# Four logit buffers in the attention, a shorter router chain, output rows scaled at the copy out, projections into the convolution from the weighted residual

## The reference

```python
# attention of a head, keys s strictly before the query t
z = q.k / sqrt(64) + b_h
log_stay = where(causal, log_sigmoid(-z), 0)
between = reverse_cumsum(log_stay) - log_stay
weight = where(causal, exp(log_sigmoid(z) + between), 0)
o = weight @ v
# convolution module
a, g = split(rmsnorm(h) @ w_in)
u = a * sigmoid(g)
y = causal depthwise conv of u, width 31; layernorm; silu; @ w_out
# experts
y[t] = sum over the two chosen e of w_sel * (silu(x @ w_gate[e]) * (x @ w_up[e])) @ w_down[e]
# the end
y = rmsnorm(h, norm_final)
```

## Time and profile before

| | us |
|---|---|
| median of three runs | 1520.71 (1519.55 to 1520.96) |
| the profiled execution | 1512.51 |
| its span, first to last instruction | 1510.8 |
| PE busy | 1337.0 (88%) |
| DVE busy | 1022.6 (68%) |
| ACT busy | 702.9 (47%) |
| POOL busy | 239.7 (16%) |
| HBM traffic | 219 GB/s over the span |

### The profile page before, as it was taken

The page is one execution under the profiler, slowest core; times in us unless marked ns, Lnnn a source line. Parts: engine busy times, 40 slices in busy tenths (PEclk is TensorE's granted clock), DMA queues, the critical chain, the costliest instruction groups (busy, mean ns, idle before and its releaser), DMA issues. The chain is left out here.

```text
span 1510.8 us, 16104 instructions
## 1 busy us (share of the span) xinstructions
PE 1337.0 (88%) x6141; PEld 1044.2 (69%) x6142; DVE 1022.6 (68%) x1071; ACT 702.9 (47%) x685; POOL 239.7 (16%) x224
## 2 busy tenths in 40 slices
PE   2899899896699999998979999899489999998893
PEld 2686355585488878886768884578478878887772
DVE  3268944315798878885754999523598878885854
ACT  1010244114477768773620007223467767785532
POOL 1033321200213323210000000100112322211000
PEclk7899899997699999999989999999599999999996
DMA  6448436207489999986460302013279999994201
GB/s 258 181 175 350 152 133 251 59 1 279 135 320 374 303 374 376 373 334 238 138 223 0 112 16 100 3 34 109 71 270 386 386 303 388 389 371 180 111 0 57
DMA packets 122740, 314.05 MB, mean 208 GB/s; under 512 B 10060, under 2 KB 10720, under 8 KB 120608
## 3 DMA queue, kind: packets, MB, share of 16 engines
q1 hardware_dynamic: 106350, 249.82, 45.8%
q0 software_dynamic: 14256, 58.69, 10.8%
q10 hardware_dynamic: 2074, 4.71, 0.9%
HBM read 304.17 MB, written 26.70 MB: 219 GB/s over the span
## 5 line engine op out<-in xcount | busy, mean ns | idle before, releaser
L1727 PE MATMUL ps<-xnT,ring 128*128 128x260 f32 x1408 | 315.8, 388 | 13.0 <-DVE xnT L1207 7.1
L1727 PEld LDWEIGHTS ps<-xnT,ring 128*128 128x128 f32 x1408 | 271.9, 193 | 56.4 <-issue 14.4
L1958 PE MATMUL ps<-ring_parts,arena_parts 128*128 128x512 f32 x768 | 308.3, 401 | 0.0
L1478 DVE TENSOR_TENSOR ring_parts<-ring,xnT_parts 128x2048 fp32r<-128x2048 f32 x96 | 219.3, 2292 | 45.1 <-ACT xnT_parts L986 44.0
L1478 DVE TENSOR_TENSOR ring_parts<-ring,arena_parts 128x2048 fp32r<-128x2048 f32 x96 | 219.4, 2291 | 40.7 <-ACT arena_parts L986 40.4
L986 ACT ACTIVATE xnT_parts<-ring 128x2048 fp32r<-128x2048 f32 x96 | 183.5, 1917 | 85.3 <-PE ps L1959 76.7
L986 ACT ACTIVATE arena_parts<-ring 128x2048 fp32r<-128x2048 f32 x96 | 183.4, 1918 | 71.7 <-PE ps L1959 48.5
L1958 PEld LDWEIGHTS ps<-ring_parts,arena_parts 128*128 128x128 f32 x768 | 148.5, 193 | 31.1
L1957 PE MATMUL ps<-xnT_parts,arena_parts 128*128 128x512 f32 x384 | 159.1, 414 | 10.1 <-DVE arena_parts L1482 10.1
L1957 PE MATMUL ps<-arena_parts 128*128 128x512 f32 x384 | 155.5, 405 | 8.9 <-DVE arena_parts L1482 5.2
L1959 PE MATMUL ps<-xnT_parts,arena_parts 128*128 128x512 f32 x384 | 155.6, 405 | 0.0
(11 more groups left out here) (283 smaller groups left out, 1704.7 us busy)
## 6 DMA issues: line engine op xcount, KB each, us to landing
ring<-in_w_gate_e SPq DMA_DIRECT2D x32, 2048.0 KB, 16.5
ring<-in_w_up_e SPq DMA_DIRECT2D x32, 2048.0 KB, 16.8
ring<-in_w_down_e SPq DMA_DIRECT2D x32, 2048.0 KB, 17.6
ring<-in_w_in_ab SPq DMA_DIRECT2D x4, 2048.0 KB, 26.7
ring<-in_w_ple_gate SPq DMA_DIRECT2D x4, 2048.0 KB, 8.1
ring<-y_rows SPq DMA_DIRECT2D x16, 512.0 KB, 6.6
ring<-in_w_in_c SPq DMA_DIRECT2D x4, 2048.0 KB, 8.7
x_rows<-arena ACTq DMA_DIRECT2D x10, 416.0 KB
```

The lines of the kernel that those rows point to most:

```text
L1478: v.tensor_tensor(w_lo, w, high[hu0 % 4].bitcast(F32), ALU.subtract).then_inc(s_lo, 1)
L1727: ins = mm(s[:, half, 0:HALF], w[:, k, :], src[:, k, half * HALF:(half + 1) * HALF], start=(k == 0), stop=(k == n - 1))
L1958: mm(ps[:, bank, :], x, w_lo, start=False, stop=False)
```

## The change

Attention. The logit buffers become four: the fourth lies over the q and k of heads already used (q and k of a head pair lie side by side now), and `LOGIT_BUF` and `LOGIT_FREE` say which head takes which buffer and for how many heads' values it waits. POOL masks the softplus of head h before the weights of h-1, and adds ahead of the sticks what lies behind each key block: two copies of 128 columns, an add of 128 and an add of 384, with a wait on its own result after the mask and after the first add. The sticks become four triangle matmuls and three with ones, 2048 columns. `values` runs once for two heads, the two 64-column halves in turn. PE's order per head is scores(h+1), sample_values(h-2), at even h values of the pair before, [wait for the subtract of h-1] turn_sample(h-3), sticks(h).

Router, both layers. The sums of squares are made per token (`token_sums`, five matmuls of 104 tokens with one column of ones), the root is over 104x5 and the five turning matmuls go. The reciprocal comes before the wait for the turned logits. The rank takes five matmuls, the selection three broadcast operations, and the row indices are written and signalled (`s_rows_of`) before the other table columns; POOL waits for these only before its first scatter.

Into the convolution. ACT writes the residual weighted by the gain (`mixed`) while the embedding still runs; PE starts cg(0) from it, the square sums follow between cg(0) and ca(0), the history's transposes after ca(0). DVE drains cg, scaling it by the reciprocal root, ACT takes the sigmoid in place, DVE scales by the reciprocal root again before the product with ca. EARLY is 13.

End. ACT writes the weighted residual (`final_rows`) during the embedding of layer 1; PE begins the transposes of the first row group, with `token_sums` before the last of them; the root is over 128x4 and 8x1, ACT scales each row at the copy out, five row buffers, and the output DMAs go from POOL's queue to the end of SP's.

```diff
-EARLY = 15
+EARLY = 13
+LOGIT_BUF = (0, 1, 2, 0, 1, 3, 2, 0)
+LOGIT_FREE = (0, 0, 0, 2, 2, 0, 4, 4)
...
-    norm(3)
-    order += [("chist", i, "dve") for i in range(2)]
     for m in range(KT):
-        order += [("cg", m, "act"), ("ca", m, "dve")]
+        order.append(("cg", m, "dve"))
+        if not m:
+            norm(3)
+        order.append(("ca", m, "dve"))
+        if not m:
+            order += [("chist", i, "dve") for i in range(2)]
...
             for h in range(SBH):
+                pool.wait_ge(s_sp, h + 1)
+                sp, later = ex[:, h % 2, :], spare[h % 2]
+                link(mask(sp))
+                pool.tensor_copy(later[:, 0:P], sp[:, 1024:1024 + P])
+                pool.tensor_copy(later[:, 256:256 + P], sp[:, 512:512 + P])
+                link(pool.tensor_tensor(later[:, P:256], sp[:, 1024 + P:1280], sp[:, 896:1024], ALU.add))
+                pool.tensor_tensor(later[:, 256 + P:640], sp[:, 512 + P:896], later[:, 0:256], ALU.add
+                                   ).then_inc(s_spm, 1)
                 if h:
                     mask_weights(h - 1)
-                pool.wait_ge(s_sp, h + 1)
-                mask(ex[:, h % 2, :]).then_inc(s_spm, 1)
...
             for h in range(SBH):
                 if h + 1 < SBH:
                     scores(h + 1)
-                if h:
-                    values(h - 1)
+                if h >= 2:
+                    sample_values(h - 2)
+                    if h % 2 == 0:
+                        values(h // 2 - 1)
                 sticks(h)
...
-                if h >= 2:
-                    turn_sample(h - 2)
+                if h >= 3:
+                    turn_sample(h - 3)
                 pe.wait_ge(s_spm, h + 1)
...
                 for kb in range(4):
-                    for src in range(kb, 4):
-                        off = (src - kb) * P
-                        width = TP - src * P
-                        ins = mm(ps_flat[:, c0 + at[kb] + off:c0 + at[kb] + off + width],
-                                 tri[:] if src == kb else ones[:], sp[:, at[src]:at[src] + width],
-                                 start=(src == kb), stop=(src == 3), skip_group_check=True)
+                    col, width = c0 + at[kb], TP - kb * P
+                    ins = mm(ps_flat[:, col:col + width], tri[:], sp[:, at[kb]:at[kb] + width],
+                             start=True, stop=(kb == 3), skip_group_check=True)
+                    if kb < 3:
+                        ins = mm(ps_flat[:, col + P:col + width], ones[:], behind[kb],
+                                 start=False, stop=True, skip_group_check=True)
...
+            def values(p):
+                pe.wait_ge(s_wm, 2 * p + 2)
...
+                    for h in (2 * p, 2 * p + 1):
+                        rows = slice(64 * (h % 2), 64 * (h % 2) + 64)
...
+                ins.then_inc(s_pv, 2)
...
+            def token_sums(i, rows, count):
...
+                for n in range(count):
+                    last = min(T, (n + 1) * rows)
+                    ins = mm(s[0:last - n * rows, 0, n:n + 1], rstd[:, n * rows:last], ones[:, 0:1], start=True, stop=True)
...
-                for n in range(10):
-                    v.tensor_scalar(sel_c[:, n, :], iot, ten(15)[:, n:n + 1], None, ALU.is_equal)
-                    ins = v.tensor_scalar(sel_b[:, n, :], iot[:, 0:NE * BLK], ten(16)[:, n:n + 1],
-                                          vl[:, n:n + 1], ALU.is_equal, ALU.mult)
-                ins.then_inc(s_sel, 1)
+                link(v.tensor_tensor(sel_b, steps_of(NE * BLK), wide(ten(16), NE * BLK), ALU.is_equal))
+                v.tensor_tensor(sel_c, steps_of(CAP), wide(ten(15), CAP), ALU.is_equal)
+                v.tensor_tensor(sel_b, sel_b, wide(vl, NE * BLK), ALU.mult).then_inc(s_sel, 1)
...
                 for m in range(KT):
+                    s = drain_wait(dve, "cg", m)
+                    v.tensor_tensor(two(csig[:, m % 2, :]), halves(s), two(rstd[:]), ALU.mult
+                                    ).then_inc(s_drained["dve"], 1)
+                    if m:
+                        sample_sums(m - 1)
+                    dve.wait_ge(s_csig, m + 1)
+                    link(v.tensor_tensor(csig[:, m % 2, :], csig[:, m % 2, :], rstd[:], ALU.mult))
                     s = drain_wait(dve, "ca", m)
...
+            def final_rows(k):
+
+                nc.scalar.activation(xnT[:, k, :], hT[:, k, :], ACT.Copy, scale=prm[:, G_FIN + k:G_FIN + k + 1]
+                                     ).then_inc(s_hg, 1)
+
+            def mixed(k):
+
+                nc.scalar.activation(xnT[:, k, :], hT[:, k, :], ACT.Copy,
+                                     scale=prm[:, G_MIX + 8 + k:G_MIX + 9 + k]).then_inc(s_xn, 1)
...
             for i in range(5):
-                if i >= 2:
-                    act.wait_ge(s_yt[i % 2], 16 * (i // 2))
                 n = P if i < 4 else TS
-                copy_out("y", i, y_tok[0:n, i % 2, :].rearrange("p (a b) -> p a b", a=2), lambda s: s[0:n, :, :])
+                s = drain_wait(act, "y", i)
+                nc.scalar.activation(y_tok[0:n, i, :].rearrange("p (a b) -> p a b", a=2), s[0:n, :, :], ACT.Copy,
+                                     scale=rstd[0:n, i:i + 1]).then_inc(s_drained["act"], 1)
```

More of the change, by code:

```diff
@@ L1108, in _ @@
                         square(3 if layer == 0 else 7, m - 2, hT)
+                        if not layer:
+                            mixed(m - 2)
+                        if layer:
+                            final_rows(m - 2)
                 if layer:
                     break
-                norm(3, "ple0", squared=KT - 2)
+                for k in range(KT - 2, KT):
+                    h_wait(act, "ple0", k)
+                    square(3, k, hT)
+                    mixed(k)
+                norm(3, "ple0", squared=KT)
                 for m in range(KT):
-                    s = drain_wait(act, "cg", m)
-                    if m >= 2:
-                        act.wait_ge(s_cu, m - 1)
-                    nc.scalar.activation(two(csig[:, m % 2, :]), halves(s), ACT.Sigmoid).then_inc(s_drained["act"], 1)
+                    act.wait_ge(s_drained["dve"], JOBS[("cg", m)][2])
+                    nc.scalar.activation(csig[:, m % 2, :], csig[:, m % 2, :], ACT.Sigmoid).then_inc(s_csig, 1)
                 copy_out("crow", 0, two(c_row), lambda s: s[0:CHIST, :, :])
@@ L1627, in _, with history @@
                     break
-                norm(3, "ple0", G_MIX + 8, added=KT - 3)
-                for i in range(2):
+                for k in range(KT - 3, KT):
+                    add_square(3, k)
+                dve.wait_ge(s_drained["act"], JOBS[("norm", 3)][2])
+                link(v.reciprocal(rstd[:], rms[:]))
+                def history(i):
                     s = drain_wait(dve, "chist", i)
@@ L1672, in _ @@
                     dve.sem_inc(s_cu, 1)
-                    if m:
+                    if not m:
+                        for i in range(2):
+                            history(i)
+                        dve.wait_ge(s_drained["dve"], JOBS[("chist", 1)][2])
+                    else:
                         taps(EARLY * (m - 1), EARLY * m)
-                    sample_sums(m)
+                sample_sums(KT - 1)
                 taps(EARLY * (KT - 1), CONV_DVE * CW)
@@ L1690, in _ @@
                 add_square(5, KT - 1)
-            norm(6, "ple1", G_FIN, added=KT - 3)
+            for k in range(KT - 3, KT):
+                add_square(7, k)
+            dve.wait_ge(s_drained["act"], JOBS[("norm", 6)][2])
+            v.reciprocal(rstd[:, 0:4], rms[:, 0:4])
+            v.reciprocal(rstd[0:TS, 4:5], rms[0:TS, 4:5]).then_inc(s_ytok, 1)
         @block.tensor
@@ L1928, in _ @@
                 pe.wait_ge(s_cnt, layer + 1)
-                for i in range(NRT):
-                    for src in range(i + 1):
-                        ins = mm(s[0:RT, 0, i * NE:(i + 1) * NE],
-                                 before[0:RT, 0:RT] if src == i else ones[0:RT, 0:RT], cnt[:, src, :],
-                                 start=(src == 0), stop=(src == i))
+                flat_cnt = cnt.rearrange("p i e -> p (i e)")
+                for far in range(NRT):
+                    ins = mm(s[0:RT, 0, far * NE:NRT * NE], ones[0:RT, 0:RT] if far else before[0:RT, 0:RT],
+                             flat_cnt[:, 0:(NRT - far) * NE], start=(far == 0), stop=(far == NRT - 1),
+                             skip_group_check=True)
                 filled(ins)
```

142 lines of the change are left out of this document (80 added, 62 removed).

## The result

The changed kernel takes 1467.6 us (median; 1464.8 to 1475.3) against 1520.8: a ratio of 0.966, interval 0.962 to 0.970, 53 us less.

What follows compares the result with a forecast made beforehand. PE paces the steady attention and expert loops; chains of steps bound the hand-over, routers and end. -4 - 4.2 - 2 - 11.5 - 12.8 = -34.5 takes the profiled 1512.5 to 1478.0 and the median 1520.7 to 1486.2 us; range 1477 to 1498.

Steps and rivals of the forecast that it cites:

- End, -12.8: End of the kernel: last output lands at 1491.7 instead of 1504.5, -12.8 us (-9.5 to -13.5).
- Attention, -4: Attention: the middle between -7.6 and -1.6 us, -4 us, range -8 to +3.
- The pauses have a price: Attention: a pause can leave PE at half clock, about 2 us lost each; three falls leave -1.6 of -7.6.
- Rival A: Attention: PE's clock falls at each pause, or POOL is dearer; 0 to +3, 1490 to 1493; chance 0.27 with E.
- Rival E: Attention: interleaved halves don't overlap and the pauses cost; attention 0, 1490; chance 0.27 together with A.
- The laid-out -7.6: Attention: its end moves by -7.6 us in the new order laid out with traced durations, before clock falls.
- D: Attention: POOL's four operations serial for 8 heads; beyond some 2 us, each microsecond costs 3 to 8, past 1520.7; chance 0.03.
- Router of layer 0, -2: Layer 0's router: same savings as layer 1, but row copies wait for x_rows; -2 us (-0.8 to -4.2).
- Router of layer 1, -4.2: Layer 1's router: reciprocal, rank, selection and row indices sum to -4.7, some lost at the gather; -4.2 us (-2.5 to -4.8).
- Convolution, -11.5: Into the convolution: earlier gate projection brings PE's means forward, taps not binding by 0.3 us; -11.5 us (-8 to -12.5).
- Rival C: Convolution: DVE's 14.0 us round has no slack, its taps end past PE's means; gain 5 only, about 1492; chance 0.12.
- B: Attention: no fall of PE's clock, attention -7.6, about 1482; chance 0.13.

Runs made afterwards that it cites:

- e_poolq: The changed kernel with its five output DMAs issued from POOL's queue instead of SP's; 1472.1 us.
- f: The changed kernel with the values of a pair's two heads issued one head after the other instead of in turn; 1474.8 us.
- g: The changed kernel with the convolution's second scaling by the reciprocal root done by POOL instead of DVE, and EARLY 14; 1473.0 us.

## Why the prediction was wrong, point by point

**End, -12.8; measured -18.6 by the means and -18.2 between the two traces.** The chain was sized right: 12.2 of the 18.2 lie ahead of the last issue. The step that failed is "what lands 2.1 us after the issue before lands at 1491.7": I took the landing as the end and carried the 6 us from it to the end of the span over as a constant. They are POOL's DRAIN behind its last transfer (e_poolq), and the change takes POOL off the end. The number stood in the trace: 1502.37 to 1510.8.

**Attention, -4; measured -9.4 by the means, -7.0 between the traces.** The step that failed is "The pauses have a price" and its "I take the middle": I charged the clock's falls, 3.6 us, to the new order only. The old order has pauses of 1.5 to 3.1 us ahead of its first values, and falls behind them in five of six executions; the execution read showed full clock behind its 1.46 and 2.14 us, and I took that for a property of the kernel. Rival A, which shares the chance of 0.27 with E, rested on the same. The laid-out -7.6 lies near the -7.0 by luck: PE waited 6.6 us ahead of the values where I had 10.0, and two falls, some 3.2 us together, gave most of it back (values 3.88 instead of 2.37, sticks 5.35 instead of 3.63). Odd heads' sticks are 25.2, 22.6 and 19.7 us apart where I had 24.6, 23.1 and 20.2. Rival E's price was right in the rivals (attention 0; f's stage is the kernel before's) but not in the term: "+0.8 on each if the halves did not overlap" is 0.2 us a pair, where a pair took 1.6 us more and the stage 9.7. D's price held: some 7 us for each microsecond of POOL, inside 3 to 8.

**Router of layer 0, -2; measured -4.7.** The row copies do still wait for x_rows (360.71, 4.66 us), but their start is 1.5 to 2.4 us closer to the residual's last tile, not 1.2, the gather's 2.6, and the gather, once released, is issued in 1.72 instead of 3.06 us, a cost that I had taken as fixed.

**Router of layer 1, -4.2; measured -5.9**, -5.3 between the traces, beyond the bound of -4.8. The steps give 1.6, 1.8, 0.95 and 1.0 = 5.3 us up to the gather where the sum had 4.7; the one mis-sized is the rank (DVE's wait 1.24, not 1.8). Behind that some was lost, as I had put it off, since DVE's passes over the first weights now end last; but the gather's issue, 1.11 instead of 2.76 us and again taken as fixed, made up for it.

**Convolution, -11.5; measured -12.7.** Near by luck, the sum of two errors: PE reached the means 15.6 us closer to the last gate product, where I had 11.7, with 1.9 of the difference from its first diagonal products, at full clock (14.01 us at 890.78) unlike in the trace of before (15.92); and DVE's taps, which I had free by 0.3 us, bound by 2.31. The 14.01 us came in all eight executions with the new code of this stage, 15.7 to 17.0 in five of the seven with the old; why is not shown. Rival C's mechanism is there, with its price far smaller.

**The 8.2 us carried over.** Of the 18.6 us between the forecast and the result only 9.5 lie in the terms: the execution was forecast at 1478.0 and took 1468.5. The other 9.1 come from "the median of the runs is 8.2 us above that, and I carry the difference over unchanged": the execution read of the kernel before was a short one, some 5 us of it from the attention's missing falls, while the changed kernel's lies 0.9 us above its median.

**Range.** Its lower end, 1477, had B and all terms at their best; a gain that is missing from a term, as at the end, was nowhere in it. Its upper end does not follow from its parts either: A at +3, C at -5 and the routers at -3.3 beside the end's -12.8 make 1502.6, not 1498.

## What to carry to other kernels

Measure a stage to the end of the span, not to the last transfer's landing, and ask of every engine that loses its last work what it did afterwards. A clock fall, or its absence, in one trace is no property of the kernel: before a new pause is charged with a price, look whether the old order has pauses of the same length, and take a second execution; a single short execution also makes a poor base for a sum. An operation on POOL costs what it takes and what it locks.

## What the runs showed of the hardware

The end of the span comes 8.1 to 8.8 us behind the start of the last issue when that is POOL's (eight executions), 2.3 to 2.7 when it is SP's (nine). POOL's DRAIN takes 5.54 to 5.55 us of the former.

DVE and POOL hold each other up. An issue of a gather that begins inside one of DVE's 2.3 us passes over two inputs ends 1.0 us behind that pass, whenever it began: 2.76 us long at 1074.94 (pass from 1074.43), 3.06 at 378.50 (from 378.31), 1.72 at 368.55 (from 367.01); the one at 1054.25 began 0.28 ahead of its pass and took 1.11. The Trainium skill, "SBUF — State Buffer" (section SBUF: two separate sides), says that the two engines share a pair of ports, which a DVE operation in a two-port mode or with two SBUF inputs, or a POOL operation, holds for the whole instruction while the other engine blocks, and that POOL can't write a transfer's descriptors during a DVE operation in a two-port mode. The gathers here, behind DVE's passes over two inputs, and DVE's 1.25 us in g agree with it in kind.

TensorE's clock can fall or not behind the same pause of the same code: behind 2.14 to 2.15 us ahead of the old attention's seventh values these took 2.37 us in three executions and 3.99 to 4.06 in three. With PE kept busy at the pauses in 206 to 228 the granted clock there went from 0.76 and 0.72 to 1.00.
